# Recurrent mixer: projections and gate products placed between the halves of the inverse, and a reordered group norm

## What is computed

```python
def rwkv7_mixer(h, mix, w_rkv, w0, w1, w2, a0, a1, a2, g1, g2, k_k, k_a, r_k, lnx_w, lnx_b, out_w):
    xs = h[None] + dx[None] * mix[:, None, None, :]
    r, k, v = jnp.einsum('nbsd,nde->nbse', xs[:3], w_rkv)
    w_log = -jax.nn.softplus(-(w0 + jnp.tanh(xs[3] @ w1) @ w2)) - 0.5
    decay = jnp.exp(-jnp.exp(w_log.astype(f32)))
    a = jax.nn.sigmoid(a0 + (xs[4] @ a1) @ a2)
    g = jax.nn.sigmoid(xs[5] @ g1) @ g2
    ...
    y = ((y - mu) * lax.rsqrt(var + R_GN_EPS)).reshape(b, s, d) * lnx_w + lnx_b
    y = (y + bonus.reshape(b, s, d)).astype(h.dtype)
    return (y * g) @ out_w
```

## Time and profile before

| | |
|---|---|
| median of 3 executions | 1745.52 us (1741.14 to 1746.62) |
| the profiled execution | 1746.13 us |
| its span in the profile | 1744.4 us |
| TensorE busy | 1671.4 us, 96% |
| VectorE busy | 1300.3 us, 75% |
| ScalarE busy | 886.4 us, 51% |
| mean granted TensorE clock | 0.992 of full speed |

### The profile page before, as it was taken

One profiled execution on the slowest core, in us unless ns is written; L12 is line 12 of the kernel. 1 busy time (PEld: TensorE's weight loads), 2 busy tenths in 40 slices (PEclk: granted clock), 3 DMA queues, 4 the chain that ended last, 5 costly groups with the idle time before them and its releaser, 6 DMA issues.

```text
span 1744.4 us, 35977 instructions
## 1 busy us (share of the span) xinstructions
PE 1671.4 (96%) x15185; PEld 1567.8 (90%) x15185; DVE 1300.3 (75%) x1914; ACT 886.4 (51%) x1254; POOL 21.6 (1%) x62
## 2 busy tenths in 40 slices
PE   7999899999999978899999998999999999999998
PEld 6998689999986866599999996999999987999998
DVE  7898887999674564579995667799958977766553
ACT  3765664544423233354454666444446768655442
POOL 4000000000000000000000000000000000000000
PEclk9999999999999999999999999999999999999999
DMA  9554457999814300139997350599964632458551
GB/s 345 170 185 137 153 187 248 338 348 346 293 58 129 128 28 3 59 120 352 355 361 268 120 160 21 197 344 357 355 223 142 186 108 97 169 166 270 178 192 67
DMA packets 217793, 347.28 MB, mean 199 GB/s; under 512 B 8416, under 2 KB 175024, under 8 KB 217632
## 3 DMA queue, kind: packets, MB, share of 16 engines
q1 hardware_dynamic: 215856, 344.22, 58.3%
q10 hardware_dynamic: 1648, 0.43, 0.1%
q0 software_dynamic: 128, 0.33, 0.1%
HBM read 343.91 MB, written 1.05 MB: 198 GB/s over the span
## 4 chain that ended last, share of the span: by engine, by line
PE 86%; DVE 7%; ACT 3%; issue 2%; DMA 2%; POOL 0%; ACTq 0%; DVEq 0%; POOLq 0%
PE psum_dve L444 30%; PE psum_act L444 29%; PE psum_acc L444 26%; DMA ring<-in_m_in_w_dram 1%; DVE arena L1603 1%; PE psum_act L447 1%; DVE w_lo L1324 1%; ACT w_hi L1851 1%; DVE arena L1467 1%; PE psum_dve L447 1%; DMA ring<-in_ada_w_dram 1%; DVE arena L1580 1%; DVE arena L1295 1%; ACT arena L1978 1%; DVE arena L1588 0%
## 5 line engine op out<-in xcount | busy, mean ns | idle before, releaser
L1851 ACT ACTIVATE w_hi<-ring 128x1024 fp32r<-128x1024 f32 x432 | 458.5, 1061 | 374.5 <-DMA ring<-in_ffn_w_dram 231.9
L1324 DVE TENSOR_TENSOR w_lo<-ring,w_hi 128x1024 fp32r<-128x1024 f32 x432 | 516.9, 1222 | 171.9 <-ACT w_hi L1851 168.8
L444 PE MATMUL psum_dve<-h_lo,w_hi 128*128 128x256 f32 x1216 | 333.0, 280 | 0.0
L444 PE MATMUL psum_act<-h_lo,w_hi 128*128 128x256 f32 x960 | 258.7, 281 | 0.0
L1295 DVE SCALAR_TENSOR_TENSOR arena<-ring,vcol,arena 128x512 f32<-128x512 f32 x336 | 239.1, 748 | 4.1 <-DMA ring<-in_ada_w_dram 0.3
L444 PEld LDWEIGHTS psum_dve<-h_lo,w_hi 128*128 128x128 f32 x1216 | 226.3, 189 | 0.2
L444 PE MATMUL psum_acc<-g_hi,w_hi 128*128 128x256 f32 x704 | 200.1, 284 | 0.0
L444 PE MATMUL psum_acc<-g_lo,w_hi 128*128 128x256 f32 x704 | 197.4, 280 | 0.0
L444 PE MATMUL psum_acc<-g_hi,w_lo 128*128 128x256 f32 x704 | 197.4, 280 | 0.0
L444 PE MATMUL psum_dve<-h_hi_ffn,w_hi 128*128 128x256 f32 x704 | 196.7, 281 | 0.1
L444 PE MATMUL psum_dve<-h_hi_ffn,w_lo 128*128 128x256 f32 x704 | 196.6, 281 | 0.0
(11 more groups left out here) (315 smaller groups left out, 3269.5 us busy)
## 6 DMA issues: line engine op xcount, KB each, us to landing
ring<-in_ffn_w_dram SPq DMA_DIRECT2D x132, 1024.0 KB, 7.1
ring<-in_ada_w_dram SPq DMA_DIRECT2D x96, 1024.0 KB, 7.1
ring<-in_m_in_w_dram SPq DMA_DIRECT2D x48, 1024.0 KB, 5.4
ring<-in_m_out_w_dram SPq DMA_DIRECT2D x16, 1024.0 KB, 5.0
ring<-in_r_w_rkv_dram SPq DMA_DIRECT2D x12, 1024.0 KB, 5.6
ring<-in_f_qkvf_w_dram SPq DMA_DIRECT2D x12, 1024.0 KB, 5.4
ring<-in_r_out_w_dram SPq DMA_DIRECT2D x4, 1024.0 KB, 5.0
ring<-in_f_out_w_dram SPq DMA_DIRECT2D x4, 1024.0 KB, 5.2
```

Source lines behind the costliest of these rows:

```text
L444: return nc.tensor.matmul(o, l, r, start=start, stop=stop, skip_group_check=True)
L1324: tell(V.tensor_tensor(o, raw, hi, ALU.subtract), split_ready, hold=False)
L1851: tell(A(o, raw, ACT.Copy), hi_ready)
```

## The change

TensorE's list. In the projections, the half of the key that goes with w2 comes before w2 in each of the four steps; only three receptance jobs stay ahead of the inverse, and `ksum` comes after the first. The fourth receptance job and `values(0)` stand between `gram` of pair 0 and `gram` of pair 1; `values(1..3)` stand in levels 1 and 2, and the gate's four products in levels 4 and 5 and behind `G` and `H`. `both(., Ki)`, the transposes and the bonus move to other levels. The load of g1 comes ahead of that of w1, a1, w2 and a2 (`lora`).

VectorE's list. The running sum starts as soon as the parts of its input are there; the factors come in another order, with the key's last factors and the bonus product inside the inverse; r is multiplied with its factor in four parts (`query`). The bonus and the norm's offset are multiplied with the gate while the chunks run (`gated_bonus`, 8 operations of 128x256).

ScalarE's list follows. The gate is weighted with `lnx_w` (8 operations of 128x256) in stage 3, a table set with sigmoid is loaded at the mixer's start, and the group norm's squares, logarithms, exponentials and roundings alternate by part. The last `outer` goes to an aux bank.

```diff
+                add(("g1",), (slice(0, 1280), rows(t["r_g1"][0], 0, LORA_G), P, LORA_G))
                 add(("lora",), ...
-                add(("g1",), (slice(0, 1280), rows(t["r_g1"][0], 0, LORA_G), P, LORA_G))
...
                 for j in range(4):
-                    b, last = open_two("act"), [None, None]
...
-                    close_two("act", *last)
                     key, u = ("rkv", 1, 2 + j // 2), j % 2
...
+                    read_out("act", mark["rwkv"][0] + 2)
+                    b, last = open_two("act"), [None, None]
...
+                    close_two("act", *last)
                 freed(("lora",), "act")
                 pe.wait_ge(xs_ready, 4)
-                for i in range(4):
-                    two_tiles_raw(("rkv", 0, i), "act", r_xsR)
...
+                two_tiles_raw(("rkv", 0, 0), "act", r_xsR)
+                note("ksum")
...
+                two_tiles_raw(("rkv", 0, 1), "act", r_xsR)
+                two_tiles_raw(("rkv", 0, 2), "act", r_xsR)
...
+                def between_pairs(lv):
+                    if lv in (3, 4):
+                        pe.wait_ge(r_v2p, 4)
+                        both(lv - 3, Ki)
+                    if lv == 1:
+                        values(1)
+                    elif lv == 2:
+                        values(3)
+                    elif lv == 3:
+                        turned(r_v)
+                    elif lv == 5:
+                        gate_pair(1)
+                        turned(r_s)
+
+                def behind_growth(lv):
+                    if lv == 1:
+                        values(2)
+                    elif lv == 2:
+                        turned(r_xsA)
+                    elif lv == 3:
+                        for j in range(4):
+                            bonus(j)
+                    elif lv == 4:
+                        gate_pair(0)
+                    else:
+                        turned(r_k)
                         each("act", 0, r_before, value)
                         each("act", 1, r_before, value)
+                        gate_pair(2)
                 pe.wait_ge(r_v2p, 2)
                 both(0, Bi)
                 N_read[0] = gram("act", 0, KKd, Bi)
-                turned(r_v)
+                two_tiles_raw(("rkv", 0, 3), "act", r_xsR)
+                values(0)
+                N_read[1] = gram("act", 1, KKd, Bi)
+                pe.wait_ge(r_v2p, 3)
                 both(1, Bi)
-                N_read[1] = gram("act", 1, KKd, Bi)
-                turned(r_xsA)
                 for lv in range(1, 6):
                     product(lv, 0)
+                    between_pairs(lv)
                     product(lv, 1)
-                    beside(lv)
                     grow(lv, 0)
                     grow(lv, 1)
+                    behind_growth(lv)
...
-                all_read_out()
+                solved = jobs["act"]
+                gate_pair(3)
+                freed(("g2",), "act")
+                read_out("act", solved)
+                read_out("dve", jobs["dve"])
...
+                head_sums(0)
+                head_sums(1)
+                square_sums(0)
+                head_sums(2)
+                square_sums(1)
+                head_sums(3)
+                square_sums(2)
+
+                def result_ready(k):
+                    if k == 2:
+                        square_sums(3)
+                    pe.wait_ge(ry_split, k // 2 + 1)
```

VectorE, the factors and the two ends of the chunks' stage:

```diff
-                dve.wait_ge(act_free, m0 + 11)
+                key_out(2)
+                key_scaled(2)
                 for k in range(KD):
+                    if k % 2 == 0:
+                        dve.wait_ge(act_free, m0 + 4 + k)
                     tell(V.tensor_tensor_scan(r_dx[:, k, :], rs, r_s[:, k, :], 0.0, ALU.mult, ALU.add))
...
+                tell(V.tensor_tensor(flat(r_xsA), flat(r_xsA), flat(r_E), ALU.mult), r_v2p)
                 dve.wait_ge(r_a2v, 7)
                 tell(V.tensor_copy(pend[:, :, :], r_dx[:, :, CH - 1:S:CH]))
...
+                query(0)
+                query(1, r_v2p)
+                tell(V.scalar_tensor_tensor(out=r_xsB[:, :, :], in0=r_a[:, :, :], scalar=-1.0, in1=wide("r_k_a", 0), ...
+                tell(V.scalar_tensor_tensor(out=flat(r_k), in0=flat(r_xsB), scalar=1.0, in1=flat(r_k), ...
+                query(2)
...
+                gated_bonus(0)
                 for c, dst in ((0, r_St[1]), (1, r_F1)):
...
                 for c in (2, 1):
...
+                for j in range(1, 4):
+                    gated_bonus(j)
                 b = take_aux()
                 give_aux(V.tensor_tensor(r_F2[:, :, :], blocks(b), ending(2), ALU.mult))
...
+                add_state(1, take(), give)
+                add_state(2, take(), give)
+                stream(rout0 + 4)
+                add_state(3, take_aux(), give_aux)
+                stream(rout0 + 5)
...
+                centred(0)
+                centred(1)
+                gated(0)
+                centred(2)
+                ended(0)
+                centred(3)
+                low(0)
+                for j in range(1, 4):
+                    gated(j)
+                    ended(j)
                     low(j)
```

More of the change, by code:

```diff
@@ L1697, in grow, with between_pairs, gated_bonus @@
                         give_aux(V.tensor_tensor(v, v, blocks(b), ALU.add))
-                def beside(lv):
-                    if lv < 3:
-                        both(lv - 1, r_before, before_c[:, :], r_upto)
-                    elif lv > 3:
-                        bonus(2 * lv - 8)
-                        bonus(2 * lv - 7)
+                def between_pairs(lv):
+                    if lv == 2:
+                        tell(V.tensor_tensor(flat(r_a), flat(r_raw), flat(r_k), ALU.mult))
+                        tell(V.tensor_tensor(flat(r_k), flat(r_k), flat(r_E), ALU.mult))
+                        tell(V.tensor_tensor(r_a[:, :, :], r_a[:, :, :], wide("r_r_k", 0), ALU.mult), r_v2p)
+                    elif lv in (3, 4):
+                        both(lv - 3, r_before, before_c[:, :], r_upto)
+                def gated_bonus(j):
+                    dve.wait_ge(act_free, mark["gate", j])
+                    for k in (2 * j, 2 * j + 1):
+                        tell(V.scalar_tensor_tensor(out=r_v[:, k, :], in0=r_v[:, k, :], scalar=col("r_lnx_b", k), in1=r_gate[:, k, :],
+                                                    op0=ALU.add, op1=ALU.mult))
                 first_inverses(0)
+                query(3, r_v2p)
                 first_inverses(1)
@@ L1709, in rwkv @@
                     product(lv, 0)
+                    between_pairs(lv)
                     product(lv, 1)
-                    beside(lv)
                     grow(0)
                     grow(1)
+                    if lv == 3:
+                        for j in range(4):
+                            bonus(j)
                 def ending(c):
@@ L2115, in rwkv @@
                     tell(A(v, v, ACT.Exp, scale=-0.5), r_a2v)
-                features(r_r, 2)
-                features(r_r, 3)
-                act.wait_ge(r_v2a, 2)
-                tell(A(flat(r_xsB), flat(r_dx), ACT.Exp, scale=E_HALF), r_a2v)
                 tell(A(flat(r_dx), flat(r_dx), ACT.Exp, scale=-E_HALF), r_a2v)
-                for j in range(4):
-                    features(r_v, j)
+                features(r_raw, 1)
+                features(r_raw, 2)
                 def blocks(b):
@@ L2129, in powers, with inverse_turned @@
                         give(A(r_N[:, 8 * u:8 * u + 8, :], blocks(b), ACT.Copy))
-                def inverse_turned():
-                    for u in range(4):
+                def inverse_turned(pair):
+                    for u in (2 * pair, 2 * pair + 1):
                         b = take()
@@ L2168, in rwkv @@
                 stream(rout0 + 2)
+                for k in range(KD):
+                    tell(A(r_wgate[:, k, :], r_gate[:, k, :], ACT.Identity, scale=col("r_lnx_w", k)), gate_weighted)
                 for c in range(NC):
```

207 lines of the change are left out of this document (107 added, 100 removed).

## The result

The changed kernel takes **1737.04 us** (median of 7 runs, 1731.02 to 1740.3) where the kernel before, run beside it, takes 1746.06 (7 runs). The ratio is 0.9957, interval 0.9937 to 0.9977. A second timing, of 12 runs beside 17, gave 0.9969 [0.9949, 0.9989]. All single times of the study together give 1737.15 in the mean for 20 runs after and 1744.9 for 37 runs before: 7.7 us, with standard errors of 0.9 and 0.7. So it is faster, by a little over half of the 14.7 us forecast.

What follows compares the result with a forecast made beforehand. TensorE, holding 86% of the span, was taken as the bound, with gain from filling its waits. Inverse -6.0, stalls +1.45, chunks +1.5, group norm -11.75 +0.95, clock -0.85: -14.7 from 1745.5, forecast 1730.8 us, range 1724.5 to 1739.

Steps and rivals of the forecast that it cites:

- Before the inverse: Projections ahead of the inverse: table-load wait of 2.31 us gone, first receptance job 4.7 us sooner, `both` at 571.4.
- the half key: First half key in the projections: without the wait ahead of it, 3.65 us instead of 5.34.
- The inverse: From `both` to the states: jobs and gates fill idle TensorE, 118.7 us, states at 690.1, 6.0 us sooner.
- Chunks and the norm: States to `down`: chunks 1.5 us later; group norm 11.75 us shorter, with 0.95 given back within `down`.
- VectorE's delay: Chunks: six `gated_bonus` pieces hold up `carry(2)` and `outer`; 1.5 us taken, bounds 0 and 2.3.
- rival (b): Group norm: clock falls, head sums take 1.9 us each, `down` starts slow; 1735.5 us, chance 0.15.
- the inverse's stalls: Four short "issue" stalls in the levels, 2.9 us together before; 1.45 us taken as remaining, bounds 0 and 2.9.
- The fall at `down`: Start of `down`: with a shorter gap ahead it may start at full clock; 0.85 us gain taken, bounds 0 and 1.7.
- (c): Inverse: VectorE's factors come late, TensorE idles 8 us more; 1738.8 us, chance 0.10.
- (d): Levels: idle time is hand-over that can't be filled, inverse takes 139 us; slower, 1751.1 us, chance 0.04.
- (a): Whole mixer: everything fits, with stalls, VectorE's delay and slow clock all gone; -18.5 us, 1727, chance 0.10.

## Why the prediction was half right

The direction, and the median within the range, came from the steps that held; the gain of 14.7 was 7.7 by the times and 8.9 by the mixer (means of three profiles each, 274.2 and 265.3).

**Before the inverse: right.** The wait of 2.31 is gone, the half key takes 3.65, and the first receptance job waits 1.22 us for ScalarE (forecast 1.15). `both` begins at 571.76 for a forecast of 571.4, with 1.14 us of waiting for VectorE (forecast 1.1). These are the two rows of the timeline.

```profile
550.08 2.18 PE L447 MATMUL psum_act<-arena,ring 128*128 128x256 f32 x9 [1.22 <-ACT arena L2165]
...
575.93 1.98 PE L447 MATMUL psum_acc<-arena 64*64 64x128 f32 x64 [1.14 <-DVE arena L1696]
```

**The inverse: prices right, stalls wrong.** Levels 3 to 5 took 14.85, 11.67 and 12.17 us for 15.1, 11.7 and 12.0; the part behind them 12.74 for 12.5; `G` and `H` 7.25, the last gate 2.12 for 2.2. Level 2 took 20.39 for 16.3: 2.90 of stall, 0.6 for transposes at the fallen clock, 0.2 in its job, and 0.3 in a wait for ScalarE ahead of it. All in all 123.51 us from `both` to the states, where 118.7 and 1.45 were forecast: 3.4 too long.

The four rows of jobs among the 64-row products took 14.07 (two jobs), 7.14, 7.11 and 7.14 us, where jobs end to end took 6.91 each: 0.9 us more for five. The rule of the Trainium skill (TensorEngine Tiling (Array Packing), Key Properties), that changing the tiling mode drains TensorE, agrees in direction. By it I had estimated some 2 us for five jobs; the rows make it half of that.

**Chunks and the norm.** From the states to `outer` it was 20.27 for a forecast of 19.75, with the stall of 3.23 over VectorE's delay and not added to it. The first `outer` was 0.5 us shorter than the 3.36 of before. From its end to `down` it was 13.73 in this profile, 2.0 above the 11.75, since the clock had fallen; 11.80 in the second profile, where it had not. `down` took 23.69, the fourth sum of squares of 0.86 included, 0.7 less than forecast. So rival (b) happened in the profiled run, but in that run alone of three (11.80 and 11.81 in the others). Of `down`, 1.4 us were gained against the 24.26 of before, where 0.85 was taken: it starts at full clock in all three profiles after and at the lower one in all three before.

These differences (0.4 + 3.4 + 0.5 - 0.5 + 2.0 - 0.7) make 5.1 us; the mixer was 5.0 above what the forecast makes of it, 276.30 - 14.7 = 261.6.

**The step that failed** is the inverse's stalls: "They sit in rows of many small products, which the jobs now break up. Bounds: all gone 0, all there 2.9; I take 1.45, knowing no reason for either." Both halves of it were wrong. The stalls depend on when blocks of instructions arrive, and I bounded them by the stalls as they stood, though the change moved frees of weight slots and with them the loads that share the DMA engines with those blocks. My count of what a moved step issues went over SyncE's queue ahead of the inverse, where it gained 4.7 us, and stopped there; the loads freed in level 2 and ahead of the states have no term in the sum, neither under the inverse nor under the chunks. Holding both back returns 5.4 us of the mixer: the two stalls, less what VectorE then adds, and the clock that fell behind them. It makes 14.3 us against the mean of before (274.2 to 259.9), beside the 14.7 forecast; that this is so near is in part luck, since the terms taken for stalls and for VectorE, 1.45 and 1.5, both came out smaller there.

**A second, smaller part** lies in the kernel before. I took single durations out of one profile, and not all of them come back: the clock fell at the half key in two of three profiles of before (5.34 and 4.19 instead of 3.65; a gain of 1.7 forecast), at the first `outer` (3.36 instead of 2.08) in that one alone, and the stalls in the levels were the longest there. The fall at `down` came in all three, so its term was no accident. In the mean of three profiles the mixer of before is 2.1 us shorter than in the first. With 265.3 - 261.6 = 3.7 that is the whole 5.8 us between 14.7 and 8.9. What lies between the mixer's 8.9 and the 7.7 of the times is within their errors.

Of the rivals, (c) did not happen (1.14 us of waiting), and (d) did not either: no product waited for a job's bank in the levels. (a) failed where the forecast did.

**Open.** Why the clock falls in one run and not in the next at the same place. Why a block waits for the end of one load and starts inside another (see below): the runs show when they start and no more. And how far ahead a block would have to be fetched for TensorE not to stand; the distance between stall and block was never varied by itself.

## What to carry to other kernels

When a step is moved, list every slot that it frees, see which load goes then, and lay that load over the places where TensorE runs many small instructions: a load there can cost more than its bytes. Hold such a load back to a stretch of large products by freeing the slot later; two moved lines gave 5 us here, and it costs nothing as long as the weights are not due. And before single durations of a profile are taken for a gain, look at a second profile of the same kernel: here that alone was 2 us of 15.

## What the hardware showed that I had not expected

- Many instruction blocks wait for loads, but not all. In 17 profiles (before, after and the runs above) 87 loads of 1 MB begin between 580 and 760 us, and 71 blocks for TensorE start between their start and just behind their end. 42 of the 71 start within 0.8 us of the load's end, and these loads last 3.4 to 4.0 us; 13 start together with the load, and 16 start inside it, 1.3 to 3.2 us behind its start, and then the load lasts 4.4 to 4.8 us. In the stalls of level 2 and of the states it was the load's end each time, 13 of 13. The stall follows where the products are small: 2.44 to 3.24 us there, against 0.4 to 1.6 for stalls without a load.
- The Trainium skill (Runtime: NRT & Kernel Launch, Instruction fetch mechanics) has the sequencer bring its instructions in 16 KB blocks on a DMA queue of its own and calls the cost of crossing a block mostly hidden. The size agrees with every block seen here. The cost does not where a weight load lies over the block: 2.90 and 3.23 us; and without one it was still up to 1.63. The skill (DMA: Bandwidth & Descriptors, Queues, rings and completion order) also has each DMA engine take turns between its queues packet by packet; by that a block should be able to start within a load. 16 of the 71 did, but 42 started only at its end, so that rule alone does not tell when a block starts.
- The granted clock fell to half right behind the stall of level 2 in all three profiles of the changed kernel, and within the levels in neither of the two with both loads held and nothing else changed. The stall does not always bring the fall: in the kernel with the old group norm it was 2.57 us at the same place, and the clock stayed at 1.00.
- Once down, it can stay down through nearly unbroken work: 0.51 over 21 us with TensorE busy for 20.06 of them, behind a stall of 1.36, in the kernel with loads in its levels. In the kernel before the fall at the same place lasted 3.4 us.
- One kernel's mixer, unchanged, took 276.30, 271.42 and 274.85 us: more than half the effect that was to be explained.
